# Key heads once in the projection weights of the two grouped attentions (640 columns, not 768), each key half written to both partition halves by ScalarE

## The chip, the cores and the metric

The kernel runs on one core of a Trainium2 chip. The metric is the device time of one execution in microseconds; three runs of the kernel before are shown, and the median counts.

## What is computed

The reference is two models in a row, on 512 tokens of width 1024, all in float32. The first has two layers of mixer and gated feed-forward. The second has two layers over 512 latent and 256 context tokens. In each of its layers one half of the mixer is a *grouped* attention: 8 query heads of 64 features share 2 key heads and 2 value heads. Layer 0 (even) has it as a banded window attention, layer 1 (odd) as a global block attention with normed and rotated queries and keys:

```python
def even_mixer(u_ctx, u_lat, w_in, w_out, a_prm, sink, rope_ang, need_ctx):
    p_ctx = u_ctx @ w_in
    p_lat = u_lat @ w_in
...
    qc, kc, vc = split_qkv(p_ctx[..., A_IN:], B_HEADS, B_KV_HEADS)
    ql, kl, vl = split_qkv(p_lat[..., A_IN:], B_HEADS, B_KV_HEADS)
...
def odd_mixer(u_ctx, u_lat, w_in, w_out, rpb, q_gain, k_gain, rope_ang, need_ctx):
...
    dq_c, dk_c, dv_c = split_qkv(p_ctx[..., C_IN:], D_HEADS, D_KV_HEADS)
    dq_l, dk_l, dv_l = split_qkv(p_lat[..., C_IN:], D_HEADS, D_KV_HEADS)
```

So a grouped projection has 512 query columns, 128 key columns (heads K0 and K1) and 128 value columns, each over a depth of 1024.

## The kernel before

**Tiles.** Tokens are counted as 768 columns, context first (256, `CTXS`) and latent behind it (512, `LAT`). A projected tensor lies with its features on the 128 partitions: `raw` of a grouped attention is `[128, 6, 768]`. Tiles 0 to 3 hold the queries, two heads in each, one on each half of the partitions. Tile 4 holds K0 on both halves and tile 5 holds K1 on both. The attention multiplies a query half by the key tile's rows of the same half (`raw[ROWS[half], j, ...]` with `k_tile(j)[ROWS[half], cols]`, and `k_tile` is `raw[:, 4 + j // 2, :]`), so that each key head must stand on both halves. For that the host function `grouped` lays the key columns out twice, 768 columns in all.

**The weight stream.** `WeightStream` brings all weights in a fixed order (`MAIN`) through a ring of 4 blocks; a block has up to 256 columns (1 MB), and SyncE loads the next one when the block 4 places before it is used up. A block is cut into pieces of 128 columns. Products are made of three float32r products: ScalarE casts a piece to its high part (`hi`), VectorE subtracts to get the low part (`lo`), into one of two slots, and TensorE multiplies high by high, high by low and low by high. `feature_products` runs over the pieces of a matrix: for each piece, for each segment of tokens, 8 row tiles by three products into one of 7 rotating banks; then it frees the piece's slot (`piece_used`).

**Side blocks.** Between the blocks of a host matrix come blocks of other matrices, the modulation weights (`SIDES`: `b_qk` and `d_qk` have three each, one behind each block of the host). VectorE multiplies such a block by two vectors and sums over its 8 row tiles (`sum_side`, 16 instructions); `sums_after` says behind which piece's `lo` this comes, for a side block behind the last piece of its host block. TensorE finishes it with 8 small products (`side_products`) behind the same piece. The modulation is read by later stages.

**The stage.** `qkv_stage` projects queries and keys piece by piece, then the values as one more piece, whose result TensorE transposes to token order. ScalarE runs in a fixed order: for piece j it first casts the weights of piece j + 1, then waits for piece j's products and copies its banks out, one copy for a segment. `b_qk` has both segments for the queries, `d_qk` only the latent one; keys and values have both in either. Behind the last copy of the values ScalarE casts the next stage's first piece (in `b_qk`), then copies the transposed values. The stage ends in a barrier of all engines. `c_qk` goes through the same function with ungrouped heads (`wide`).

Of the kernel before, what the change touches and what calls it, by code (L numbers as in the profile page):

```python
# [24 lines left out]
ACT = mybir.ActivationFunctionType  # L25
# [5 lines left out]
P = 128  # L31
# [21 lines left out]
HD = 64  # L53
# [16 lines left out]
NROT = 7  # L70
# [3 lines left out]
def feature_plan(n_cols, k_tiles=DK, width=256):  # L74

    return [(0, k_tiles, c, min(width, n_cols - c)) for c in range(0, n_cols, width)]


def token_plan(n_cols, k_tiles):

    return [(k, min(4, k_tiles - k), c, 512) for c in range(0, n_cols, 512) for k in range(0, k_tiles, 4)]
# [8 lines left out]
    ("up0", feature_plan(2 * FFN)), ("down0", token_plan(D, FK)),  # L90
    ("cv_in", feature_plan(2 * D)), ("cv_out", token_plan(D, DK)),
    ("up1", feature_plan(2 * FFN)), ("down1", token_plan(D, FK)),
    ("b_qk", feature_plan(768)), ("b_v", feature_plan(P, width=P)),
    ("lora", feature_plan(256) + [(0, DK, 256, P)]),
    ("rkv0", feature_plan(768)), ("rkv1", feature_plan(768)),
    ("out0", token_plan(D, DK)), ("ff1_0", feature_plan(DFF)), ("ff2_0", token_plan(D, DFF // P)),
    ("c_qk", feature_plan(1024)), ("c_v", token_plan(512, DK)),
    ("d_qk", feature_plan(768)), ("d_v", feature_plan(P, width=P)),
    ("out1", token_plan(D, DK)), ("ff1_1", feature_plan(DFF)), ("ff2_1", token_plan(D, DFF // P)),
]  # L100
ADAS = {"ada_mix0": ADA1, "ada_ffn0": ADA1, "ada_mix1": ADA1, "ada_ffn1": ADA1, "ada0": ADA2, "ada1": ADA2}
# [258 lines left out]
def build(nc, dram, out_dram, debug=None):  # L360

    psum = nc.alloc_psum_tensor("banks", [P, NBANK * BANK], F32)
    ps = [psum[:, i * BANK:(i + 1) * BANK] for i in range(NBANK)]
# [15 lines left out]
    @contextmanager  # L379
    def stage():  # L380
        with nc.cleanup_on_exit():  # L381
            yield
# [1146 lines left out]
    def flat_of(x):  # L1529

        return x[:].rearrange("p a b -> p (a b)")
# [180 lines left out]

    def qkv_stage(qk_name, v_name, hT, raw, n_q, vtok, q_segs, q_scale=1.0, then=None):

        n_k = raw.shape[1] - n_q
        v_cols = vtok.shape[2]
        wide = v_cols == BANK
        v_feat = flat_of(gate_rows)[:, 0:TOK]
        segs_of = lambda j: q_segs if j < n_q else [CTXS, LAT]
        with stage():  # L1720
            mm_done, copied, turned = sem("mm_done"), sem("copied"), sem("v_turned")
            first = weights.at["pe"]
            N = n_q + n_k
            n_copies = sum(len(segs_of(j)) for j in range(N))
            with nc.Block() as block:
                @block.sync
                def _(sp):
                    weights.load(sp, v_name)

                @block.tensor  # L1730
                def _(pe):
                    g = feature_products(pe, qk_name, hT, segs_of, copied)
                    if wide:
                        token_products(pe, v_name, all_tiles, lambda p, kk, i: tuple(
                            h[:, 2 * p + kk, i * P:(i + 1) * P] for h in hT), mm_done, copied, g0=g)
                    else:
                        g = feature_products(pe, v_name, hT, [CTXS, LAT], copied, g0=g)
                        pe.wait_ge(copied, g)
                        for t in all_tiles:
                            last = nc.tensor.transpose(ps[t // 4][:, (t % 4) * P:(t % 4 + 1) * P], v_feat[:, t * P:(t + 1) * P], ident[:])  # L1740
                        last.then_inc(turned, 1)

                @block.scalar
                def _(act):
                    g, hi_left = 0, N + (DK // 2 if wide else 1)
                    weights.hi(act)
                    hi_left -= 1
                    for j in range(N + (0 if wide else 1)):
                        if hi_left:
                            weights.hi(act)  # L1750
                            hi_left -= 1
                        act.wait_ge(weights.piece_used, first + j + 1)
                        for s in segs_of(j):
                            to = raw[:, j, s] if j < N else v_feat[:, s]
                            nc.scalar.activation(to, ps[g % NROT][:, 0:s.stop - s.start], ACT.Copy, scale=q_scale if j < n_q else 1.0).then_inc(copied, 1)
                            g += 1
                    if wide:
                        for _ in range(hi_left):
                            weights.hi(act)
                        if then is not None:  # L1760
                            weights.hi_early(act, then)
                        for t in all_tiles:
                            act.wait_ge(mm_done, t + 1)
                            nc.scalar.copy(vtok[:, t, :], ps[(g + t) % NROT][:]).then_inc(copied, 1)
                    else:
                        if then is not None:
                            weights.hi_early(act, then)
                        act.wait_ge(turned, 1)
                        nc.scalar.copy(vtok[:, 0:4, :], ps[0][:].rearrange("p (t d) -> p t d", d=P))
                        nc.scalar.copy(vtok[:, 4:TOK_T, :], ps[1][:, 0:2 * P].rearrange("p (t d) -> p t d", d=P))  # L1770

                @block.vector
                def _(dve):
                    for _ in range(N + (DK // 2 if wide else 1)):
                        weights.lo(dve)
                    if then is not None:
                        weights.lo_early(dve, then)
                    side_sums(dve, qk_name, v_name)
# [1434 lines left out]
def lay_out(i):  # L3213
    plans = dict(WEIGHTS)
    out = lay_out_first(i)
    i = {k: np.asarray(v) for k, v in i.items()}
    out.update(second_constants())
    unit = np.ones((P, DK), np.float32)
    for l in range(DEPTH):
        pre_mix, post_mix, pre_ff, post_ff = (columns(i[n][l]) for n in ("g_pre_mix_2", "g_post_mix_2", "g_pre_ff_2", "g_post_ff_2"))  # L3220
        out[f"gains_ada{l}"] = np.ascontiguousarray(np.concatenate([unit, pre_mix, post_mix, unit, pre_ff, post_ff], axis=1))
    for l in range(DEPTH):
        out[f"ada{l}"] = blocks_of(i["w_ada_2"][l], ADA2)
        out[f"out{l}"] = blocks_of(i["w_out_2"][l], plans[f"out{l}"])
        out[f"ff1_{l}"] = blocks_of(i["w_ff1_2"][l], plans[f"ff1_{l}"])
        out[f"ff2_{l}"] = blocks_of(i["w_ff2_2"][l], plans[f"ff2_{l}"])
    even, odd = i["w_in_even_2"][0], i["w_in_odd_2"][0]

    def grouped(w):

        k0, k1 = w[:, 512:512 + HD], w[:, 512 + HD:512 + 2 * HD]
        return np.concatenate([w[:, :512], k0, k0, k1, k1], axis=1), w[:, 640:768]

    qk, v = grouped(even[:, 1920:])
    out["b_qk"], out["b_v"] = blocks_of(qk, plans["b_qk"]), blocks_of(v, plans["b_v"])
    qk, v = grouped(odd[:, 1536:])
    out["d_qk"], out["d_v"] = blocks_of(qk, plans["d_qk"]), blocks_of(v, plans["d_v"])
    out["c_qk"], out["c_v"] = blocks_of(odd[:, :1024], plans["c_qk"]), blocks_of(odd[:, 1024:1536], plans["c_v"])
    out["lora"] = blocks_of(even[:, 1536:1920], plans["lora"])
    for h in range(2):  # L3240
        cols = [even[:, x * 512 + h * 256:x * 512 + (h + 1) * 256] for x in range(3)]
        out[f"rkv{h}"] = blocks_of(np.concatenate(cols, axis=1), plans[f"rkv{h}"])
    mu = np.stack([columns(i["a_mu_prev_2"][0]), columns(i["a_mu_next_2"][0])], axis=-1).reshape(P, 30)
    two = lambda x: np.concatenate([columns(x[0]), columns(x[1])], axis=1)
    out["r_cols"] = np.ascontiguousarray(np.concatenate([
        mu, two(i["a_w0_2"][0]), two(i["a_a0_2"][0]), columns(i["a_k_k_2"][0]), columns(i["a_k_a_2"][0]),
        columns(i["a_r_k_2"][0].reshape(-1)), columns(i["a_gn_w_2"][0]), columns(i["a_gn_b_2"][0])], axis=1))
    for name, src in (("w2", i["a_w2_2"][0]), ("a2", i["a_a2_2"][0])):
        full = np.zeros((2, P, 2, 2 * P), np.float32)
        for d in range(2):  # L3250
            for h in range(2):
                full[h, d * HD:(d + 1) * HD, d] = src[d][:, h * 256:(h + 1) * 256]
        out[name] = full
    out["g2"] = np.ascontiguousarray(i["a_g2_2"][0].reshape(P, 2, 2 * P).transpose(1, 0, 2))
    out["b_sink"] = i["b_sink_2"][0]
    out["rpb_table"] = rpb_layout(i["c_rpb_2"][0])
    out["d_gain"] = np.ascontiguousarray(np.stack([np.tile(i["d_q_gain_2"][0], 2), np.tile(i["d_k_gain_2"][0], 2)], axis=1))
    return out
# [13 lines left out]
```

## Time and profile before

| | us |
|---|---|
| runs of the kernel before | 3687.14, 3688.95, 3690.34 |
| their median | 3688.95 |
| span of the profiled execution, first to last instruction | 3684.6 |
| b_qk and b_v, TensorE's first product to the next stage's | 1339.8 to 1408.4 |
| d_qk and d_v | 2966.6 to 3022.7 |

The profiled execution's own device time is not listed beside its span; the median of the runs is 4.35 us above that span. A profile row names the line, the engine, the operation and the tile that is written and read. PE is TensorE, PEld its weight loads, DVE VectorE, ACT ScalarE, SP SyncE. Times in a timeline are from the start of the span. A matmul's duration includes its way through the array, so that the distance between two starts is what one costs.

### The profile page before, as it was taken

What the parts mean: (1) busy time and instruction counts of PE and PEld (TensorE: products, weight loads), DVE (VectorE), ACT (ScalarE), POOL (GpSimd) and SP (SyncE); (2) the same over time, 40 slices, a digit from 0 to 9 for tenths busy, and PEclk for the clock granted to TensorE, in tenths of its full rate; (3) what the DMA queues carried; (4) which work ended last, traced back from release to release, by engine and by line L of the source; (5) the groups of instructions that cost most, each with busy time, mean ns of one, the idle gap of its engine ahead of it and who ended that gap; (6) DMA issues with size and microseconds to landing.
All of it is one profiled execution on the core that took longest, in us unless ns stands there. A gap on an engine that the chain in (4) does not pass through costs nothing. (4 is left out here: it accounts for less than half of the span.)

```text
span 3684.6 us, 62774 instructions
## 1 busy us (share of the span) xinstructions
PE 3230.6 (88%) x26414; PEld 2617.1 (71%) x26414; DVE 2201.8 (60%) x3942; ACT 1289.6 (35%) x2191; POOL 139.9 (4%) x180
## 2 busy tenths in 40 slices
PE   6989998988999958976776777999998999879999
PEld 5767876646887757844765766887887777658787
DVE  7678866785786466766445445554334556663344
ACT  2333334334333332154324325222234225642243
POOL 0200001000000001000101100000000000000000
PEclk8989999998999979988988998999999999989999
DMA  7524462202335212310000022322221242022231
GB/s 291 166 105 182 183 182 88 69 12 78 135 137 138 99 48 105 125 53 30 5 32 12 5 72 82 113 103 98 75 92 58 103 138 70 1 97 92 82 96 69
DMA packets 64424, 342.67 MB, mean 93 GB/s; under 512 B 15120, under 2 KB 16656, under 8 KB 28432
## 3 DMA queue, kind: packets, MB, share of 16 engines
q1 hardware_dynamic: 61616, 326.82, 26.1%
q0 software_dynamic: 2528, 11.84, 0.9%
q8 instruction: 209, 3.42, 0.4%
q14 instruction: 71, 0.58, 0.1%
HBM read 327.84 MB, written 10.79 MB: 92 GB/s over the span
## 5 line engine op out<-in xcount | busy, mean ns | idle before, releaser
L263 DVE TENSOR_TENSOR weight_lo<-weight_ring,weight_hi 128x1024 fp32r<-128x1024 f32 x341 | 423.0, 1242 | 152.5 <-ACT weight_hi L248 147.6
L248 ACT CAST weight_hi<-weight_ring 128x1024 fp32r<-128x1024 f32 x341 | 355.9, 1044 | 177.4 <-PE banks L420 91.9
L418 PE MATMUL banks<-hT_hi.1,weight_hi 128*128 128x512 f32 x896 | 365.9, 408 | 24.8 <-PEq L381 22.7
L419 PE MATMUL banks<-hT_lo.1,weight_hi 128*128 128x512 f32 x896 | 358.8, 400 | 0.0
L420 PE MATMUL banks<-hT_hi.1,weight_lo 128*128 128x512 f32 x896 | 358.5, 400 | 0.0
L418 PEld LDWEIGHTS banks<-hT_hi.1,weight_hi 128*128 128x128 f32 x896 | 171.4, 191 | 68.2 <-issue 25.7
L419 PEld LDWEIGHTS banks<-hT_lo.1,weight_hi 128*128 128x128 f32 x896 | 171.3, 191 | 41.5 <-issue 1.9
L420 PEld LDWEIGHTS banks<-hT_hi.1,weight_lo 128*128 128x128 f32 x896 | 171.0, 191 | 41.9
L418 PE MATMUL banks<-hT_hi.3,weight_hi 128*128 128x512 f32 (+1 forms) x512 | 175.5, 343 | 7.9 <-PEq L381 7.9
L419 PE MATMUL banks<-hT_lo.3,weight_hi 128*128 128x512 f32 (+1 forms) x512 | 174.3, 341 | 0.0
L420 PE MATMUL banks<-hT_hi.3,weight_lo 128*128 128x512 f32 (+1 forms) x512 | 174.3, 340 | 0.0
L317 DVE SCALAR_TENSOR_TENSOR side_sum<-weight_ring,silu_c2.1,side_sum 128x256 f32<-128x256 f32 x336 | 160.3, 477 | 0.0
L317 DVE SCALAR_TENSOR_TENSOR weight_ring<-weight_ring,silu_c2.1 128x256 f32<-128x256 f32 x336 | 160.2, 477 | 0.0
L517 PE MATMUL banks<-weight_hi,left_hi.6 128*128 128x512 f32 x360 | 144.5, 401 | 8.3 <-DVE weight_lo L263 8.3
L520 PE MATMUL banks<-weight_lo,left_hi.6 128*128 128x512 f32 x360 | 142.5, 396 | 0.0
L519 PE MATMUL banks<-weight_hi,left_lo.6 128*128 128x512 f32 x360 | 141.9, 394 | 0.0
L317 DVE SCALAR_TENSOR_TENSOR weight_ring<-weight_ring,silu_c1.1 128x256 f32<-128x256 f32 x280 | 135.6, 484 | 10.5
L418 PE MATMUL banks<-hT_hi.2,weight_hi 128*128 128x256 f32 (+1 forms) x352 | 123.6, 351 | 17.1 <-PEq L381 17.1
L420 PE MATMUL banks<-hT_hi.2,weight_lo 128*128 128x256 f32 (+1 forms) x352 | 122.0, 347 | 0.0
L419 PE MATMUL banks<-hT_lo.2,weight_hi 128*128 128x256 f32 (+1 forms) x352 | 122.0, 346 | 0.0
L262 DVE TENSOR_TENSOR left_lo.6<-ff_hidden.1,left_hi.6 128x1536 fp32r<-128x1536 f32 x24 | 42.2, 1760 | 130.9 <-ACT weight_hi L248 130.9
L2666 ACT COPY residual.1<-banks 128x512 f32<-128x512 f32 x120 | 70.3, 586 | 140.6 <-PE banks L2824 139.4
(744 smaller groups left out, 7759.1 us busy)
## 6 DMA issues: line engine op xcount, KB each, us to landing
weight_ring<-ff SPq DMA_DIRECT2D x64, 1024.0 KB, 4.9
weight_ring<-ada SPq DMA_DIRECT2D x48, 1024.0 KB, 5.0
weight_ring<-up SPq DMA_DIRECT2D x44, 1024.0 KB, 6.9
weight_ring<-ada_ffn SPq DMA_DIRECT2D x24, 1024.0 KB, 5.0
weight_ring<-down SPq DMA_DIRECT2D x20, 1024.0 KB, 4.9
weight_ring<-ada_mix SPq DMA_DIRECT2D x16, 1024.0 KB, 4.9
first_blocks.1<-ada_mix SPq DMA_DIRECT2D x8, 1024.0 KB, 11.8
weight_ring<-cv_in SPq DMA_DIRECT2D x8, 1024.0 KB, 5.0
```

Of the source, the lines that this page charges most:

```text
L248: self.nc.scalar.copy(hi, raw).then_inc(self.hi_made, 1)
L262: self.nc.vector.tensor_tensor(x[2], x[0], x[1].bitcast(F32), ALU.subtract)
L263: self.nc.vector.tensor_tensor(lo, raw, hi.bitcast(F32), ALU.subtract).then_inc(self.lo_made, 1)
L317: ins = self.nc.vector.scalar_tensor_tensor(out=to, in0=w[:, k, :], scalar=vec[:, k, v:v + 1], in1=to, op0=ALU.mult, op1=ALU.add)
L418: nc.tensor.matmul(out, w_hi, x_hi, start=first, stop=False)
L419: nc.tensor.matmul(out, w_hi, x_lo, start=False, stop=False)
L420: return nc.tensor.matmul(out, w_lo, x_hi, start=False, stop=last)
L517: one = nc.tensor.matmul(out, xh, hi[:, kk, :], start=(k == 0), stop=False)
L519: nc.tensor.matmul(out, xl, hi[:, kk, :], start=False, stop=False)
L520: last = nc.tensor.matmul(out, xh, lo[:, kk, :], start=False, stop=(k == k_tiles - 1))
L2666: nc.scalar.copy(XT_flat[c % 2], pair(c, X_AT, 4 * CH)).then_inc(xt_copied[c % 2], 1)
```

## The change

The host function `grouped` takes the key columns once (K0 and K1 side by side, 640 columns with the queries). `b_qk` and `d_qk` have blocks of 256, 256 and 128 columns and five pieces. In `qkv_stage` a grouped attention has one key piece. When its products are in, ScalarE writes for each segment four copies of 64 partitions each: rows 0 to 63 of the bank (K0) to both halves of tile 4, and rows 64 to 127 (K1) to both halves of tile 5. The last of the four signals `copied` for that bank. `raw` and all that reads it are as before.

```diff
--- before.py
+++ after.py
@@ -90,12 +90,12 @@
     ("up0", feature_plan(2 * FFN)), ("down0", token_plan(D, FK)),
     ("cv_in", feature_plan(2 * D)), ("cv_out", token_plan(D, DK)),
     ("up1", feature_plan(2 * FFN)), ("down1", token_plan(D, FK)),
-    ("b_qk", feature_plan(768)), ("b_v", feature_plan(P, width=P)),
+    ("b_qk", feature_plan(640)), ("b_v", feature_plan(P, width=P)),
     ("lora", feature_plan(256) + [(0, DK, 256, P)]),
     ("rkv0", feature_plan(768)), ("rkv1", feature_plan(768)),
     ("out0", token_plan(D, DK)), ("ff1_0", feature_plan(DFF)), ("ff2_0", token_plan(D, DFF // P)),
     ("c_qk", feature_plan(1024)), ("c_v", token_plan(512, DK)),
-    ("d_qk", feature_plan(768)), ("d_v", feature_plan(P, width=P)),
+    ("d_qk", feature_plan(640)), ("d_v", feature_plan(P, width=P)),
     ("out1", token_plan(D, DK)), ("ff1_1", feature_plan(DFF)), ("ff2_1", token_plan(D, DFF // P)),
 ]
 ADAS = {"ada_mix0": ADA1, "ada_ffn0": ADA1, "ada_mix1": ADA1, "ada_ffn1": ADA1, "ada0": ADA2, "ada1": ADA2}
@@ -1712,9 +1712,13 @@
 
     def qkv_stage(qk_name, v_name, hT, raw, n_q, vtok, q_segs, q_scale=1.0, then=None):
 
-        n_k = raw.shape[1] - n_q
         v_cols = vtok.shape[2]
         wide = v_cols == BANK
+
+
+        n_k = raw.shape[1] - n_q if wide else 1
+        spread_k = [(0, 0, 0), (0, 1, 0), (1, 0, 1), (1, 1, 1)]
+        rows_of = (slice(0, HD), slice(HD, P))
         v_feat = flat_of(gate_rows)[:, 0:TOK]
         segs_of = lambda j: q_segs if j < n_q else [CTXS, LAT]
         with stage():
@@ -1751,8 +1755,14 @@
                             hi_left -= 1
                         act.wait_ge(weights.piece_used, first + j + 1)
                         for s in segs_of(j):
-                            to = raw[:, j, s] if j < N else v_feat[:, s]
-                            nc.scalar.activation(to, ps[g % NROT][:, 0:s.stop - s.start], ACT.Copy, scale=q_scale if j < n_q else 1.0).then_inc(copied, 1)
+                            bank = ps[g % NROT][:, 0:s.stop - s.start]
+                            if n_q <= j < N and not wide:
+                                for tile, dst, src in spread_k:
+                                    last = nc.scalar.copy(raw[rows_of[dst], n_q + tile, s], bank[rows_of[src]])
+                                last.then_inc(copied, 1)
+                            else:
+                                to = raw[:, j, s] if j < N else v_feat[:, s]
+                                nc.scalar.activation(to, bank, ACT.Copy, scale=q_scale if j < n_q else 1.0).then_inc(copied, 1)
                             g += 1
                     if wide:
                         for _ in range(hi_left):
@@ -3228,8 +3238,7 @@
 
     def grouped(w):
 
-        k0, k1 = w[:, 512:512 + HD], w[:, 512 + HD:512 + 2 * HD]
-        return np.concatenate([w[:, :512], k0, k0, k1, k1], axis=1), w[:, 640:768]
+        return w[:, :640], w[:, 640:768]
 
     qk, v = grouped(even[:, 1920:])
     out["b_qk"], out["b_v"] = blocks_of(qk, plans["b_qk"]), blocks_of(v, plans["b_v"])
```

## Rows read from the trace of the kernel before

**Rows 1.** Page, part 1: busy us, share of the span, instructions

```profile
PE 3230.6 (88%) x26414; PEld 2617.1 (71%) x26414; DVE 2201.8 (60%) x3942; ACT 1289.6 (35%) x2191; POOL 139.9 (4%) x180
```

**Rows 2.** Busy time cut into windows, b_qk stage; the first row names columns

```profile
core 0: us, PE busy (x) PEld busy (x) DVE busy (x) ACT busy (x) POOL busy (x), PEclk, DMA share, GB/s
1339.80:1351.00 11.20, 11.13 (x49) 10.04 (x50) 7.38 (x17) 1.05 (x1) 0.00 (x0) 0.75 0.29 96
1386.40:1394.70 8.30, 8.30 (x51) 7.22 (x49) 1.30 (x2) 1.79 (x4) 0.00 (x0) 1.00 0.01 2
1394.70:1404.00 9.30, 9.26 (x55) 7.84 (x54) 0.00 (x0) 0.86 (x2) 0.00 (x0) 1.00 0.46 169
```

**Rows 3.** Timeline of TensorE, key piece K1 of b_qk; start, us

```profile
1386.17 0.28 PE L418 MATMUL banks<-hT_hi.2,weight_hi 128*128 128x256 f32 x1
...
1393.79 0.40 PE L418 MATMUL banks<-hT_hi.2,weight_hi 128*128 128x512 f32 x1
1394.03 0.39 PE L419 MATMUL banks<-hT_lo.2,weight_hi 128*128 128x512 f32 x1
...
1394.49 0.28 PE L429 MATMUL banks<-ones.1,side_sum 128*128 128x1 f32 x2
...
1395.30 0.36 PE L418 MATMUL banks<-hT_hi.2,weight_hi 128*128 128x256 f32 x1
```

**Rows 4.** Timeline of TensorE, key piece K1 of d_qk

```profile
3000.97 0.28 PE L418 MATMUL banks<-hT_hi.4,weight_hi 128*128 128x256 f32 x1
...
3009.41 0.28 PE L429 MATMUL banks<-ones.1,side_sum 128*128 128x1 f32 x2
```

**Rows 5.** Waits, 1339 to 1408 us: total us, times, longest

```profile
PE banks L418 <- PEq L381: 7.9, 1, 7.9
...
PE banks L1740 <- ACT gate_rows.1 L1755: 1.0, 1, 1.0
```

**Rows 6.** Timeline of ScalarE, b_qk stage from 1377 us

```profile
1377.90 1.05 ACT L248 CAST weight_hi<-weight_ring 128x1024 fp32r<-128x1024 f32 x1
1386.37 0.87 ACT L1755 ACTIVATE qk_b.1<-banks 128x256 f32<-128x256 f32 x2 [7.42 <-PE banks L420]
1387.13 1.05 ACT L248 CAST weight_hi<-weight_ring 128x1024 fp32r<-128x1024 f32 x1
1394.69 0.87 ACT L1755 ACTIVATE qk_b.1<-banks 128x256 f32<-128x256 f32 x2 [6.51 <-PE banks L420]
1404.00 0.87 ACT L1755 ACTIVATE gate_rows.1<-banks 128x256 f32<-128x256 f32 x2 [8.44 <-PE banks L420]
```

**Rows 7.** Groups by line and form, ScalarE, 1340 to 1408 us: mean ns

```profile
L1755 ACT ACTIVATE qk_b.1<-banks 128x512 f32<-128x512 f32 x6 | 3.6, 593 | 0.0
L1755 ACT ACTIVATE qk_b.1<-banks 128x256 f32<-128x256 f32 x6 | 2.3, 383 | 44.7 <-PE banks L420 44.7
```

**Rows 8.** Timeline of VectorE, d_qk stage

```profile
2988.65 1.22 DVE L263 TENSOR_TENSOR weight_lo<-weight_ring,weight_hi 128x1024 fp32r<-128x1024 f32 x1
2993.45 1.23 DVE L263 TENSOR_TENSOR weight_lo<-weight_ring,weight_hi 128x1024 fp32r<-128x1024 f32 x1 [3.58 <-ACT weight_hi L248]
2994.59 0.35 DVE L315 TENSOR_SCALAR side_sum<-weight_ring,silu_c2.1 128x256 f32<-128x256 f32 x1
...
3000.39 0.48 DVE L317 SCALAR_TENSOR_TENSOR weight_ring<-weight_ring,silu_c2.1 128x256 f32<-128x256 f32 x1
```

**Rows 9.** Timeline of SyncE's queue, d_qk stage

```profile
2980.46 0.33 SPq L219 DMA_DIRECT2D weight_ring<-ada  x1
```

**Rows 10.** DMA issues by line, 2966 to 3022 us: count, KB, us to landing

```profile
weight_ring<-ada SPq DMA_DIRECT2D x3, 1024.0 KB, 5.4
```

**Rows 11.** Waits of TensorE, whole kernel: total us, times, longest

```profile
PE banks L418 <- PEq L381: 62.7, 10, 7.9
```

**Rows 12.** Busy time in a window, the scan stages; columns as rows 2

```profile
1566.00:2280.00 714.00, 523.68 (x13348) 434.07 (x13348) 374.72 (x973) 294.46 (x707) 53.49 (x110) 0.90 0.11 36
```

**Rows 13.** Mean granted clock of TensorE over the span

```profile
core 0: 3684.6 us, clock 0.941
```

## The prediction

> **What bounds the kernel now.** I read the busy shares first: TensorE is busy for 3230.6 of the 3684.6 us span, 88% of it, while ScalarE and VectorE are far below it [rows 1]. A share of the whole kernel says nothing about the two stages that the change touches, so the second view is the busy time cut at the piece borders of the first grouped stage (b_qk with b_v, some 68 us of the span). A piece is 128 weight columns: TensorE is busy in 8.30 of 8.30 us of the sixth key-and-query piece and in 9.26 of 9.30 us of the value piece that follows, both at granted clock 1.00 (the 2.4 GHz level). In the sixth piece VectorE works 1.30 us and ScalarE 1.79 us, and hardly any data is moved [rows 2]. Third, the waits of that stretch: inside the stage TensorE waits only at its start, behind the barrier (7.9 us), and for 1.0 us ahead of the transposes at its end, for ScalarE's copy of the values [rows 5]. No matmul of a piece waits for a weight, a bank or a transfer. So TensorE's stream of products sets the length of the stage, and what is taken out of that stream in the middle comes off the end, if ScalarE's new work stays inside its idle time.
>
> **What is removed.** The key heads stand in the weights twice, so tiles 4 and 5 of the six are a piece of K0|K0 and one of K1|K1. After the change there is one piece K0|K1 in each of the two grouped stages (b_qk and d_qk). A key piece covers 8 row tiles, 3 products, 2 segments (256 context and 512 latent tokens): 8 x 3 x 2 = 48 matmuls with 48 weight loads. In b_qk the sixth piece's first matmul starts at 1386.17 and the side product behind its last one at 1394.49: 8.32 us [rows 3]. In d_qk the same two marks are 3000.97 and 3009.41: 8.44 us [rows 4]. Both pieces are keys over both segments, so the removed work is the traced one and not a mean of mixed shapes (a query piece of d_qk has only 24 matmuls). The sum of the gain is 8.32 + 8.44 = 16.76 us.
>
> The trace spaces two 512-column matmuls of this piece by 0.24 us (1393.79 to 1394.03) [rows 3], and the 8.32 us are with such spacings. The Trainium skill, "TensorE: Matmul & The Clock Gate", section "Back-to-back issue gap", gives about 131 ns for sustained 512-column matmuls and, for an isolated one, columns over 2.4 GHz plus 2.5 ns, which is 109 ns at 256 columns; with the one for 24 matmuls and the other for 24 the two pieces would be worth 2 x (24 x 0.131 + 24 x 0.109) = 11.5 us. The trace does not agree, and since it times the very instructions that go, 16.76 us stands.
>
> **What goes with it at no price.** One weight split in each stage goes: a cast on ScalarE (about 1.05 us) and a subtraction on VectorE (about 1.22 us). Both engines wait for TensorE here, so this is worth nothing. The third weight block is 512 KB where it was 1024 KB; nothing in the stage waits for a transfer [rows 5], so nothing again. The number of blocks stays at three for each stage, so the same number of side blocks (parts of the modulation product, summed on VectorE) goes with them, and their side products stay on TensorE: 0.81 us from 1394.49 to 1395.30 [rows 3] is kept.
>
> **What is added on ScalarE.** The key piece is now read out eight times in half height (two segments, two tiles, two halves) where each of the two old pieces was read out twice in full height. A full-height copy takes 383 ns with 256 columns and 593 ns with 512 [rows 7]; the pair of them takes 0.76 us until the next instruction starts (1386.37 to 1387.13) [rows 6]. No row shows a copy of 64 partitions, nor one that moves values to the other half. Bounds: at half price the eight take 4 x 0.38 = 1.5 us; one after the other without any overlap 4 x (0.383 + 0.593) = 3.9 us. I take 4 x 0.76 = 3.0 us, by the same line's own pair, since a row of 256 or 512 columns is still walked over in full. This lies beside TensorE's side products and value piece: from the start of the key copies to that of the value copies there are 9.31 us (1394.69 to 1404.00) in which ScalarE does nothing but 0.87 us of copies [rows 6]. The next weight cast is not queued behind the key copies: the value piece's cast is issued ahead of them, in the place of the one at 1377.90 [rows 6]. What is queued behind them is the pair of value copies, and TensorE's transposes wait for those. So the added copies cost nothing up to 9.31 us in all, 1.16 us for each, three times the 256-column row. No matmul bank waits either: in b_qk the value piece's banks only ask for copies of the third query piece. Cost on the path: 0, between 0 and 0. Below nothing is excluded, since the path does not run through this engine.
>
> **What is moved on VectorE.** The third side sum came after the sixth subtraction and now comes after the fifth, and the value piece's subtraction comes behind it. I look at d_qk, where query pieces are short and VectorE is tighter. The fifth subtraction starts at 2988.65 and takes 1.22 us; the side sum ran from 2994.59 to 3000.39 + 0.48 = 3000.87, that is 6.28 us [rows 8]. Put together it runs from 2989.9 to 2996.2, and TensorE asks for it at 3000.97, the end of the key piece: 4.8 us to spare. The value piece's subtraction is then over by 2997.4 and is asked for at about 3001.8, after the side products. Its cast takes the place of the cast that released the subtraction at 2993.45 [rows 8]. The sum needs its side block: issued at 2980.46 [rows 9], 5.4 us to land [rows 10], there at 2985.9, 4.0 us ahead. On SyncE the later loads wait either for what is unchanged in time or for events that come one piece earlier. So nothing here is late, and the cost is 0. If this cover were gone, TensorE would stand still at the side products by the time that is missing, at most 8.4 us in a stage.
>
> **After the stages.** Each ends at a barrier and the next begins with weights that are in the ring already; those loads were issued before the border or come earlier with it. The attentions read the same four copies of the keys from the same places. So the shift is carried to the end. The profiled execution's span goes from 3684.6 to 3667.8 us. The median of the runs shown is 3688.95 us, 4.35 us above that span; I keep this distance: 3688.95 - 16.76 = 3672.2 us.
>
> **The rivals.**
> (a) *One stage gives its gain back*: a side sum, a transfer or ScalarE is late by a piece there. Speaking for it: only that VectorE's work of two blocks now stands closer together in d_qk. Against it: the 4.8 and 4.0 us to spare. Time: 3688.95 - 8.4 = 3680.6 us.
> (b) *The copies across partition halves are dear.* From 9.31 us on they push the value copies, the transposes and the barrier. The gain is gone when eight take 9.31 + 8.38 = 17.7 us, 2.2 us each, four to six times the rows of full height [rows 7]. Time 3689 us; the same time stands for the case that products are not in fact taken out. Nothing speaks for either.
> (c) *The clock, slower than before.* TensorE starts each stage at the lower level: the first piece of b_qk had granted clock 0.75 over 11.20 us, where a warm piece needs 8.3 [rows 2]. There are ten such starts of the projections alone [rows 11], and the scan stages further on run at 0.90 in the mean over 714 us with TensorE at 524 busy [rows 12]. If the shift by one piece changes what the clock does behind each barrier and in the scan, the mean clock moves. TensorE's 3230.6 us at 0.941 mean clock [rows 1, 13] are worth 3.4 us for each 0.001. The gain is gone when the mean falls by 0.005, and the kernel is slower by over 7.4 us when it falls by 0.007, to 0.934: 3696.4 us. Against it: the three runs, in which the clock had its own freedom, lie within 3.2 us.
> (d) *The clock, the other way*: a mean higher by 0.002 gives 3665 us.
> The Trainium skill, same page, section "What's actually happening", says that the activity monitor behind the clock is free-running and that the number of slow matmuls at a start varies from run to run; by that rule (c) and (d) would be scatter and not a step, and no row of one profile can show it.
>
> **How the numbers follow.** The forecast, both pieces off the path, has a chance of 0.82; its own range is 3667 to 3678 us: 16.76 us with 5 us on either side, for scatter of the clock (the 3.2 us between runs and the 2.7 us that one cold first piece costs). Rival (a) has 0.06, (b) 0.04, (c) 0.03, (d) 0.05. The range is 3667 to 3679 us; it leaves out most of (a) to (d), 0.18. A measurement can tell about 0.2% from no change, 7.4 us, so that the border of faster is 3681.6 us: faster 0.82 + 0.06 + 0.05 = 0.93, the same 0.04, slower 0.03.
>
> **What would show it.** TensorE's instructions fall by 96, each grouped stage has five projection pieces ahead of the value piece, and b_qk's stage is shorter by 8.3 us and d_qk's by 8.4. ScalarE shows eight copies in a row of about 0.38 and 0.59 us in each, done 6 us ahead of the value copies. TensorE's wait ahead of the transposes stays at 1.0 us; if it grows, (b) is at work. A wait of the side products for VectorE would be (a). If the stages shrink as said and the time does not, the mean granted clock tells whether it is (c), and the stretches between the marks tell where. The prediction is wrong if copies to the other half cost over 1.16 us each or if a stage behind the barriers was waiting for something that did not move with it.

## The result, and the profile after

The changed kernel took 3669.78 us in the median of four runs (3668.07 to 3672.60), the kernel before 3689.64 us in that session: a ratio of 0.9947 with a 95% interval of 0.9935 to 0.9959, that is 19.9 us less (15 to 24). The forecast was 3672.2 us, a gain of 16.8.

The page of the changed kernel, its head and part 1; it answers [rows 1]:

```profile
span 3668.9 us, 62580 instructions
...
PE 3212.3 (88%) x26318; PEld 2598.4 (71%) x26318; DVE 2200.5 (60%) x3940; ACT 1292.5 (35%) x2197; POOL 139.9 (4%) x180
```

TensorE lost 96 matmuls (26414 to 26318) and 18.3 us of busy time. ScalarE has six instructions more (sixteen half-height copies in place of eight full-height ones, and two casts fewer).

The timeline of ScalarE in the b_qk stage of the changed kernel (start us, duration us); it answers [rows 6]:

```profile
1379.16 1.05 ACT L248 CAST weight_hi<-weight_ring 128x1024 fp32r<-128x1024 f32 x1
1387.71 3.89 ACT L1761 COPY qk_b.1<-banks 64x256 f32<-64x256 f32 x8 [7.50 <-PE banks L420]
1396.94 0.87 ACT L1765 ACTIVATE gate_rows.1<-banks 128x256 f32<-128x256 f32 x2 [5.34 <-PE banks L420]
1397.70 1.05 ACT L283 CAST weight_hi<-weight_ring 128x1024 fp32r<-128x1024 f32 x1
```

The eight copies stand in a row, 3.89 us, and ScalarE is then idle for 5.34 us until the value products are ready. The value piece's cast (1379.16) is ahead of them. The waits of the same stage of the changed kernel (total us, times, longest), which answer [rows 5]:

```profile
PE banks L418 <- PEq L381: 7.9, 1, 7.9
...
PE banks L1744 <- ACT gate_rows.1 L1765: 1.0, 1, 1.0
```

They are what they were: 7.9 us at the barrier, 1.0 us ahead of the transposes. TensorE has no new wait. The timeline of VectorE in the d_qk stage of the changed kernel; it answers [rows 8]:

```profile
2982.67 1.22 DVE L263 TENSOR_TENSOR weight_lo<-weight_ring,weight_hi 128x1024 fp32r<-128x1024 f32 x1
2983.81 0.35 DVE L315 TENSOR_SCALAR side_sum<-weight_ring,silu_c2.1 128x256 f32<-128x256 f32 x1
...
2990.00 1.22 DVE L263 TENSOR_TENSOR weight_lo<-weight_ring,weight_hi 128x1024 fp32r<-128x1024 f32 x1
2995.97 0.17 DVE L449 TENSOR_TENSOR modulation_ada1.1<-banks,bias_ada1.1 128x6 f32<-128x6 f32 x1 [4.75 <-PE banks L429]
```

The fifth subtraction, the third side sum and the value piece's subtraction (2990.00) follow each other without a pause, and VectorE then waits 4.75 us for the side products behind the key piece.

**Where the time went.** The program has barriers, and TensorE's first instruction behind each is a mark that both kernels have. Lengths between marks, in us, for the kernel before, and the difference to it in each profile taken since (the two of the further version are given in its paragraph):

| stretch | before | after | both_again | both_third | both_fourth | before_again | b_only | d_only | copies_alone | copies_x4 |
|---|---|---|---|---|---|---|---|---|---|---|
| b_qk stage | 68.52 | -8.41 | -8.56 | -8.43 | -8.35 | -0.04 | -8.33 | +0.02 | -0.02 | -1.62 |
| lora stage | 35.70 | -0.91 | -1.04 | -0.91 | -0.89 | -0.01 | -0.88 | 0.00 | -0.01 | -0.86 |
| d_qk stage | 56.04 | -8.47 | -8.48 | -8.48 | -8.46 | -0.01 | +0.02 | -8.47 | +0.01 | -1.05 |
| all the rest | 3524.4 | +2.1 | -4.6 | -6.5 | -8.1 | -4.1 | +1.9 | +0.6 | +1.9 | -0.1 |
| span | 3684.64 | -15.7 | -22.7 | -24.3 | -25.8 | -4.2 | -7.3 | -7.9 | +1.9 | -3.6 |

The first three rows repeat to 0.2 us in profiles of one kernel. The fourth does not: it moves by 4.1 us between two profiles of the kernel before (before and before_again), by 6.0 us if copies_alone, whose three stages have their old lengths, is taken in, and by 10 us among the four of the changed one.

### The profile page after: what moved, and what is told of

Its sections match the earlier page's. It is cut to its first block and busy times, and to the rows that moved or that the text cites. A ratio compares the mean times of both kernels' runs of the same rounds, so it can differ in the third digit from the quotient of the medians.

```text
span 3668.9 us, 62580 instructions
## 1 busy us (share of the span) xinstructions
PE 3212.3 (88%) x26318; PEld 2598.4 (71%) x26318; DVE 2200.5 (60%) x3940; ACT 1292.5 (35%) x2197; POOL 139.9 (4%) x180
## 5 line engine op out<-in xcount | busy, mean ns | idle before, releaser
L418 PE MATMUL banks<-hT_hi.1,weight_hi 128*128 128x512 f32 x896 | 365.2, 408 | 25.7 <-PEq L381 23.5
```

Of the source, the lines that this page charges most:

```text
L418: nc.tensor.matmul(out, w_hi, x_hi, start=first, stop=False)
```

## The experiments

Ten runs were made in three sessions; each session has its own runs of the kernel before to compare with. The edits are shown against the changed kernel, in cuts marked by dots.

| | ratio to before | 95% interval | difference of the medians, us |
|---|---|---|---|
| both_again | 0.9936 | 0.9923 to 0.9948 | -23.5 |
| b_only | 0.9974 | 0.9964 to 0.9983 | -10.0 |
| copies_alone | 0.9996 | 0.9988 to 1.0005 | -1.0 |
| copies_x4 | 0.9985 | 0.9976 to 0.9994 | -6.5 |
| both_third | 0.9938 | 0.9925 to 0.9950 | -24.6 |
| d_only | 0.9981 | 0.9972 to 0.9990 | -6.6 |
| before_again | 0.9999 | 0.9990 to 1.0008 | +0.3 |
| values_first | 0.9939 | 0.9926 to 0.9953 | -23.0 |
| both_fourth | 0.9938 | 0.9925 to 0.9950 | -22.7 |
| values_second | 0.9945 | 0.9931 to 0.9959 | -21.3 |

**The changed kernel again.** No edit.

> The changed kernel itself, unaltered, against the kernel before, to size the effect. First theory: only the two removed key pieces count, 8.3 + 8.4 = 16.8 us, a ratio of 0.9954; the 19.9 us between the first medians are partly scatter of the clock. Rival: something else gives another 3 us, then the ratio stays at 0.9946 or below and the stretches outside the two stages are shorter by 3 us in sum.

Measured: 23.5 us, and the interval (19 to 28) leaves 16.8 out. The two stages were shorter by 8.56 and 8.48 us, the lora stage between the changed places by 1.04. So the pieces are worth what was said, and something more is there.

**One stage alone.** In b_only the second host layout and the second stage stay as before:

```diff
-    ("d_qk", feature_plan(640)), ("d_v", feature_plan(P, width=P)),
+    ("d_qk", feature_plan(768)), ("d_v", feature_plan(P, width=P)),
...
-        n_k = raw.shape[1] - n_q if wide else 1
+        once = qk_name == "b_qk"
+        n_k = 1 if once else raw.shape[1] - n_q
...
-                            if n_q <= j < N and not wide:
+                            if n_q <= j < N and once:
```

> Only b_qk has its key heads once, d_qk keeps 768 columns and six pieces. If the gain is the piece taken out of each stage and nothing further on, this gives half of it: 8.4 us of the kernel before (ratio 0.9977), the b_qk stage shorter by 8.4 us, the d_qk stage as before (56.0 us from its first product to the first score of the attention). Rival, that the shift itself changes the clock or the stages behind: the gain would be away from half of both_again by more than 2 us.

Measured: -10.0 us (6 to 13), b_qk stage -8.33, d_qk stage unchanged. It is half of the 19.9 of the first session, but both_again's half would be 11.8; that is 1.8 away, just within its bound of 2 us. d_only is the mirror of it (640 columns and one key piece in d_qk alone).

> Only d_qk has its key heads once; b_qk keeps 768 columns. Pieces alone: 8.4 us, ratio 0.9977, and with b_only the two make up the whole. Rival, an extra behind the d_qk stage: 12 to 14 us, ratio 0.9965, and the stretch from the ungrouped attention's start to the next attention's is 113 to 117 us, against 119 in the kernel before and in b_only.

Measured: -6.6 us (4 to 10), d_qk stage -8.47, and from the ungrouped attention's start to the next one's 120.9 us. That speaks against an extra behind d_qk: a kernel that has the whole change there has the longest such stretch of the profiles, and copies_alone (next paragraph), whose d_qk stage keeps its length, has one of 115.0 us. The two ratios multiply to 0.9955, 16.6 us, which is the sum of the forecast; with the intervals of both put together that is 12 to 21 us.

**ScalarE's part alone.** The weights keep 768 columns, laid out as queries, K0|K1, K0|K1; all six pieces are multiplied, and of the sixth one column of each bank is read:

```diff
-    ("b_qk", feature_plan(640)), ("b_v", feature_plan(P, width=P)),
+    ("b_qk", feature_plan(768)), ("b_v", feature_plan(P, width=P)),
...
-        n_k = raw.shape[1] - n_q if wide else 1
+        n_k = raw.shape[1] - n_q
...
-                            if n_q <= j < N and not wide:
+                            if j == n_q and not wide:
...
+                            elif j == n_q + 1 and not wide:
+                                col = 0 if s.start == 0 else 1
+                                nc.scalar.copy(spare[:, col:col + 1], bank[:, 0:1]).then_inc(copied, 1)
...
-        return w[:, :640], w[:, 640:768]
+        return np.concatenate([w[:, :640], w[:, 512:640]], axis=1), w[:, 640:768]
```

> ScalarE's part alone: the weights stay at 768 columns with K0|K1 twice and all six pieces are multiplied, the first key piece is read out by the eight half-height copies, and of the second one only one column of each bank is read. If the copies are hidden, the time is that of the kernel before within 2 us (ratio 0.9995 to 1.0005). Rival, that eight copies in a row (3.9 us) hold up something: slower than before by up to 2 x 3 us, ratio 1.0015 or more.

Measured: -1.0 us, with an interval that holds 1. The stages have their old lengths to 0.02 us. So the eight copies are hidden here. They stand one piece earlier than in the changed kernel, and what is queued behind them is the value piece's cast (at 1392.09, right behind the last copy) and not the value copies; that they are hidden in their real place too is read from the changed kernel's own wait ahead of the transposes, 1.0 us as before. What the two stages became shorter is then the removed products.

**The limit of the cover.** Each of the eight copies is done four times, one waiting for the other:

```diff
                                 for tile, dst, src in spread_k:
+                                    for _ in range(3):
+                                        nc.scalar.copy(raw[rows_of[dst], n_q + tile, s], bank[rows_of[src]]).then_inc(again, 1)
+                                        repeats[0] += 1
+                                        act.wait_ge(again, repeats[0])
                                     last = nc.scalar.copy(raw[rows_of[dst], n_q + tile, s], bank[rows_of[src]])
```

> The changed kernel, but every one of the eight half-height copies is done four times, one behind the other. The prediction's limit: they are free up to 9.3 us in a stage. 32 copies take 16 x 0.38 + 16 x 0.59 = 15.5 us, with the waits between them up to 18 us, so the value copies come 6.3 to 8.7 us late and the kernel is 12.6 to 17.4 us slower than both_again: about the time of the kernel before. TensorE's wait ahead of the transposes grows from 1.0 us to 7 to 10 us in each stage. Rival, that ScalarE has more room than thought (its copies are not what the transposes wait for): within 3 us of both_again.

Measured: 16.9 us slower than both_again in the same session (3682.9 against 3666.0), inside the 12.6 to 17.4 expected. The timeline of ScalarE in the b_qk stage of copies_x4, first key copies, last one, value copies:

```profile
1386.07 1.16 ACT L1763 COPY qk_b.1<-banks 64x256 f32<-64x256 f32 x3 [7.42 <-PE banks L420]
...
1401.51 0.58 ACT L1766 COPY qk_b.1<-banks 64x512 f32<-64x512 f32 x1
1402.11 0.87 ACT L1770 ACTIVATE gate_rows.1<-banks 128x256 f32<-128x256 f32 x2
```

and the wait of TensorE ahead of the transposes there:

```profile
PE banks L1745 <- ACT gate_rows.1 L1770: 7.7, 1, 7.7
```

32 copies take 16.0 us (1386.07 to 1402.11); TensorE waits 7.7 us where it waited 1.0. The cover is real and has an end: 16.0 less the 6.7 us of added wait leaves 9.3 us that are free, which is the 9.31 us read off [rows 6]. The wait in the d_qk stage is 7.7 us as well. Per stage the price over both_again was 6.9 and 7.4 us, 14.4 in all; the other 2.5 of the 16.9 us lie outside the two stages.

**The kernel before against itself, and the changed one a third and a fourth time.**

> The kernel before, unaltered, against itself: what the timing shows where nothing is changed, and a second profile of it. Scatter theory: ratio 1 within its interval, and the stretch from the ungrouped attention to the next one, 119.2 us in the first profile, comes out anywhere between 113 and 119. Rival, extra behind the changed d_qk stage: that stretch is 119 again within 1 us.

> The changed kernel once more, beside d_only and the kernel before in one session, since the gain came out at 19.9 and 23.5 us and not 16.8. The two removed pieces measured 8.4 and 8.5 us in the traces; in the traces so far the stretches between barriers elsewhere differ by up to 6 us from one profile to the next, in kernels that are the same there. If the rest is this scatter, the ratio comes back towards 0.9954 and, over the three sessions, lies between 0.994 and 0.9955. Rival: a true extra of 3 to 6 us behind the d_qk stage (the ungrouped attention and the norm stage), then the ratio is 0.9945 or below again.

> The changed kernel a fourth time, as the neighbour of values_second in one session and for the size of the gain. The pieces give 16.8 us and the earlier rise of the clock behind the b_qk stage 0.9 us, 17.7 in all (0.9952); the three sessions so far gave 19.9, 23.5 and 24.6 us. If the rest is scatter, this one comes out at 0.994 to 0.9955, and the profile shows the lora stage 0.9 us shorter again, with the clock's rise 3.1 to 3.5 us behind its start, not 5.3.

Measured: before_again has the ratio 0.9999 and a second profile whose span is 4.2 us shorter than the first; from the ungrouped attention to the next 118.3 us, so by its own bound of 1 us this run did not tell scatter from an extra. both_third and both_fourth gave 0.9938 twice. For both_third that falls on the side of its rival, an extra of 3 to 6 us (0.9945 or below), though not at the place that it named: d_only and copies_alone speak against that. Both are a little below the 0.994 to 0.9955 that scatter alone would have given, and their intervals end at 0.9950, short of the 0.9952 of the parts. So in three of four sessions the gain is 22.7 to 24.6 us, and the parts make 17.7. The lora stage of both_fourth was 0.89 us shorter, as expected.

**A further version.** values_first has the value piece first, then the key piece, then the queries; the transposes of the values are issued ahead of the last query piece, and the next stage's first cast ahead of its copies:

```diff
-    ("b_qk", feature_plan(640)), ("b_v", feature_plan(P, width=P)),
+    ("b_v", feature_plan(P, width=P)), ("b_qk", feature_plan(640)),
...
+                    def turn(piece):
+                        if piece != n_q - 1:
+                            return
+                        pe.wait_ge(copied, G + 2 - NROT)
+                        for t in all_tiles:
+                            last = nc.tensor.transpose(turned_to[t // 4][:, (t % 4) * P:(t % 4 + 1) * P], v_feat[:, t * P:(t + 1) * P], ident[:])
+                        last.then_inc(turned, 1)
+
+                    g = feature_products(pe, v_name, hT, [CTXS, LAT], copied)
+                    feature_products(pe, qk_name, hT, lambda piece: segs_of(piece + 1), copied, g0=g, after_piece=turn)
...
+                        if j == n_pieces - 1:
+                            if then is not None:
+                                weights.hi_early(act, then)
+                            act.wait_ge(turned, 1)
```

> A further version: the value piece comes first in both grouped stages, then the key piece, then the queries; the transposes of the values are issued ahead of the last query piece and the next stage's first weight cast too. In the changed kernel 4.4 us (b) and 3.7 us (d) lie between the end of the value products and the next stage's first product: copies, transposes, copies, cast and split, barrier. Behind a query piece only its copy, the side products, the modulation's sum and the barrier are left: some 2.4 us in each. Theory: another 3.3 us faster than the changed kernel. Rival, VectorE's third side sum now ends last in d_qk, where three short query pieces follow each other: then the gain there is gone and the whole is within 1.5 us of the changed kernel or slower.

> The version with the value piece first again, since one session gave it the same time as the changed kernel although its trace has three places that are shorter: b_qk stage by 2.6 us, lora stage by 1.6 us (TensorE's pause at the barrier is short and the clock stays at its upper level), d_qk stage by 1.6 us. Theory: 5 to 6 us faster than both_fourth, ratio 0.9925 to 0.9945. Rival: the same places are shorter and the time is not, because what is saved comes back in the scan and attention stages, whose lengths move by some us with the clock; then within 2 us of both_fourth.

Measured: values_first was expected to gain another 3.3 us, from the two stages alone. The places are shorter in both profiles, by more than that: against the kernel before, the b_qk stage by 10.98 and 10.98 us, the lora stage by 2.50 and 2.49, the d_qk stage by 10.04 and 9.99, some 5.7 us in all beyond the changed kernel. The time is not: 0.9939 beside 0.9938 for both_third, 0.9945 beside 0.9938 for both_fourth. In the profiles the second half of the scan took, first both_fourth, then values_second (busy time cut at the barriers; columns as rows 2):

```profile
1902.24:2144.11 241.87, 175.79 (x6152) 153.10 (x6153) 114.02 (x281) 88.09 (x213) 24.79 (x52) 0.92 0.06 18
```

```profile
1901.88:2148.41 246.53, 175.12 (x6152) 153.89 (x6153) 114.37 (x281) 87.89 (x213) 24.38 (x52) 0.92 0.06 18
```

4.7 us longer with the same instructions and the same busy time, so what was saved is not seen in that profile's span; the first half of the scan adds another 3.7 us. Two profiles cannot say that it is always so: the kernel before (245.6 us) and copies_alone (246.0) have a second half as long. The version is no better than the changed kernel within what these runs can tell.

## Why the prediction was right, and where it was short

**The removed pieces**: right. 8.32 and 8.44 us were read off the kernel before [rows 3, 4]; the stages shrank by 8.35 to 8.56 and 8.46 to 8.48 us in four profiles, and by 8.33 and 8.47 us where one stage was changed alone. The estimate from the Trainium skill's spacing ("TensorE: Matmul & The Clock Gate", "Back-to-back issue gap") was 11.5 us for both; the trace and the runs, with 16.8 to 17.0 us, disagree with it.

**What goes at no price, and VectorE's move**: right. No new wait of TensorE. The third side sum was expected to end 4.8 us ahead of its need in d_qk. It ended by 2990.00, where the next subtraction starts, and ScalarE's first key copy, right behind the key products, starts at 2995.18: some 5 us. The sum itself began at 2983.81 without a pause, so its side block had landed.

**ScalarE's copies**: the cost on the path (0) and the limit (9.31 us) were right, the size was not: 3.0 us were taken, and 3.89 us measured, the upper bound. The mis-sized step is "by the line's own pair": full-height copies of two banks start 0.28 us apart where one takes 0.38, the half-height ones do not. Three of them in the changed kernel, one by one:

```profile
1387.71 0.37 ACT L1761 COPY qk_b.1<-banks 64x256 f32<-64x256 f32 x1 [7.50 <-PE banks L420]
...
1388.09 0.36 ACT L1761 COPY qk_b.1<-banks 64x256 f32<-64x256 f32 x1
...
1388.47 0.37 ACT L1761 COPY qk_b.1<-banks 64x256 f32<-64x256 f32 x1
```

They start 0.38 us apart. Two more views of the same trace narrow down why: the fourth and fifth copies together, and the two full-height copies of the transposed values.

```profile
1388.85 0.97 ACT L1761 COPY qk_b.1<-banks 64x256 f32<-64x256 f32 x2
...
1398.78 0.59 ACT L1779 COPY v_b.1<-banks 128x512 f32<-128x512 f32 x1
1399.26 0.38 ACT L1780 COPY v_b.1<-banks 128x256 f32<-128x256 f32 x1
```

The fourth and fifth read different banks and still take 0.97 us together, no less than 0.367 + 0.582, so it is not the shared bank. The last two are plain copies of full height and start 0.48 us apart where the first takes 0.59, so it is not the other instruction either. What is left of these is the half height; no run changed it alone. It costs nothing here.

**"I keep this distance"**: this step was wrong in its reason. The 4.35 us between span and median were taken as something that lies around the span. In the changed kernel the profiled run has its own time beside its span, 3670.81 and 3668.9 us, and in its other three runs too the time is 1.9 us above the span. The profiled execution of the kernel before was then one of some 3686.5 us, 2.4 us below the median of its runs. Set against that, the first profile pair shows a gain of only 15.7 us. A single span is a sample of what moves by some us. The forecast of the median was not hurt by it: the gain is taken off the median of the runs, and the distance drops out.

**"So the shift is carried to the end"**: this is the step that fell short. The stage right behind b_qk, lora, became 0.9 us shorter in every profile with a shortened b_qk stage (six of those in the table) and by 0.01 us or less in the others. Nothing was changed in it. Its first piece in the kernel before and in d_only, busy time in the first 5.5 us (columns as rows 2; the last but two is the granted clock):

```profile
1408.39:1413.90 5.51, 5.51 (x25) 5.49 (x26) 4.60 (x12) 1.05 (x1) 0.00 (x0) 0.52 0.70 198
```

```profile
1410.35:1415.90 5.55, 5.55 (x26) 5.51 (x27) 4.64 (x12) 1.05 (x1) 0.00 (x0) 0.52 0.67 207
```

the same in the changed kernel, in copies_x4 and in values_second:

```profile
1401.35:1406.90 5.55, 5.55 (x29) 5.35 (x30) 4.65 (x12) 1.04 (x1) 0.00 (x0) 0.69 0.70 211
```

```profile
1406.50:1412.00 5.50, 5.50 (x29) 5.32 (x30) 4.60 (x12) 1.05 (x1) 0.00 (x0) 0.68 0.65 213
```

```profile
1399.34:1404.90 5.56, 5.56 (x36) 5.07 (x37) 4.65 (x12) 1.05 (x1) 0.00 (x0) 1.00 0.92 323
```

The granted clock is at its lower level (1.2 GHz) early in this stage and rises to 2.4 GHz on the way: 5.3 us behind the start in the kernel before, before_again, d_only and copies_alone, 3.1 to 3.5 us behind it in the four profiles of the changed kernel, in b_only and in copies_x4. It fell 1.5 us ahead of the start in the first group, and in the changed kernel and b_only between 0.3 us ahead of it and 0.05 us behind it. The granted clock is 0.50 throughout 1406.90:1413.72 in the kernel before and 1401.40:1404.81 in the changed one, 6.8 and 3.4 us. The rise can be seen in the starts of the 256-column matmuls, which go from 0.21 to 0.12 us apart; in the changed kernel:

```profile
1404.42 0.41 PE L420 MATMUL banks<-hT_hi.2,weight_lo 128*128 128x256 f32 x1
1404.64 0.36 PE L418 MATMUL banks<-hT_hi.2,weight_hi 128*128 128x256 f32 x1
1404.84 0.28 PE L419 MATMUL banks<-hT_lo.2,weight_hi 128*128 128x256 f32 x1
1404.96 0.28 PE L420 MATMUL banks<-hT_hi.2,weight_lo 128*128 128x256 f32 x1
```

1.8 to 2.2 us sooner at double speed is 0.9 to 1.1 us, against a measured difference of 0.86 to 1.04. copies_x4, whose b_qk stage is shorter by only 1.62 us, shows it too, so it does not grow with the length that is saved; there the clock had already fallen 6.7 us ahead of the start, in TensorE's long wait for ScalarE. Every kernel with the early rise also lacks the sixth piece in b_qk, so no run separates the shift of the stage's end from the missing piece itself. In values_second the clock did not fall at that barrier: another 1.6 us. The end of the b_qk stage and the start of the next in the changed kernel, then the start in values_second:

```profile
1397.87 0.88 PE L1744 MATMUL banks<-identity.1,gate_rows.1 128*128 128x128 f32 x6 [0.96 <-ACT gate_rows.1 L1765]
1401.35 0.50 PE L418 MATMUL banks<-hT_hi.2,weight_hi 128*128 128x256 f32 x1 [2.60 <-PEq L381]
```

```profile
1399.34 0.36 PE L418 MATMUL banks<-hT_hi.2,weight_hi 128*128 128x256 f32 x1 [1.38 <-PEq L381]
```

TensorE paused 1.4 us there and not 2.6. But the transposes are gone from that place as well: the changed kernel has 4.4 us between its last product and the next stage's first, of which 0.9 us are transposes. Which of the two kept the clock up was not tried. The forecast had the clock as rivals (c) and (d) and took it for scatter; at this place it is a step that repeats. The Trainium skill, "TensorE: Matmul & The Clock Gate", section "What's actually happening", has the monitor free-running and the count of slow matmuls varying from run to run; over ten profiles the rise at this place has two groups and not a spread, so the trace does not agree with it here, while in the scan and the ungrouped attention, below, the lengths do vary.

**What stays open.** The pieces and the lora stage make 17.7 us. The medians say 20 to 25 in four sessions. Between the two lies "all the rest" of the table: -8.1 to +2.1 us in the changed kernel, -4.1 to +1.9 us in the three profiles whose stages have their old lengths. A large part of it is in two stretches, the scan's second half (241.4 to 246.8 us) and the one from the ungrouped attention to the next (113.4 to 120.9 us). For the second, d_only and then both_fourth:

```profile
3012.77:3133.65 120.88, 103.96 (x884) 80.81 (x885) 78.29 (x201) 62.90 (x139) 7.58 (x6) 0.87 0.25 76
```

```profile
3001.61:3115.38 113.77, 98.14 (x885) 75.93 (x885) 78.22 (x201) 62.80 (x139) 7.59 (x6) 0.92 0.26 80
```

Same instructions, mean granted clock 0.87 and 0.92: TensorE's busy time differs by 5.8 of the 7.1 us. So in this pair the stretch goes with the clock. That the shift moves the clock there on average in the changed kernel's favour fits the medians, but b_only and d_only together show only 16.6 us, and with four profiles against three it is argued, not shown. Within one session the step from b_only to both_again was 13.5 us and the one from d_only to both_third 18.0 us, where a piece makes 8.5 and a piece with the lora stage's share 9.3; so the extra appears where both stages are changed, and no run says why. The mean clock over all runs of a kernel in a session does not settle it: 0.9428 against 0.9427 for the kernel before in the session of both_again, 0.9436 against 0.9425 with both_third and 0.9432 against 0.9428 with both_fourth, for gains of 23.5, 24.6 and 22.7 us.

That the first time fell well inside the range of 3667 to 3679 us is in part luck. Taken off the 3688.95 us from which the forecast started, the gains of the three later sessions would be 3664.4 to 3666.3 us, just below it. The terms that were read off the rows are right; what is beyond them had been put at nothing but scatter.

**The rivals.** (a), a stage gives its gain back: did not happen, and its cover of 4.8 us was found. (b), dear copies: refuted by copies_alone and by the unchanged wait of 1.0 us; copies_x4 shows where it would begin. (c), slower by the clock: no. (d), faster by the clock: the 0.9 us are of this kind, and perhaps the rest.

The price that (c) and (d) put on the clock, 3.4 us for each 0.001 of the mean, is not borne out. The profile of the changed kernel has 0.943 where the one before has 0.941, which at that price would be 6.9 us on top of the pieces, and the spans differ by 15.7 us, less than the pieces. In the session of both_again ten runs of the kernel before share the mean 0.942 and lie between 3684.0 and 3695.3 us. Two smaller sums of the prediction are off, without weight for the forecast: a mean lower by 0.007 makes the kernel slower by 7.3 us at its own price, not by over 7.4, and a cold first piece costs 11.20 - 8.3 = 2.9 us by its own rows, not 2.7.

## What to carry to other kernels

Read a removal off the very instructions that go, with starts and not durations, and check it by the length between two barriers, which repeats to 0.2 us where the whole kernel moves by 5 us or more. Give an added chain of copies the time until the next thing that is queued behind it, and test the limit by multiplying the chain: here the 9.3 us of cover were found again to 0.1 us. And where TensorE pauses at barriers, look at the granted clock behind the next barrier as a term of its own: its rise there moved by 2 us with the stage ahead, and in the version with a pause of 1.4 us and no transposes ahead of it, it did not fall at all.

## What the runs showed of the hardware

A ScalarE copy of 64 partitions takes nearly as long as one of 128: 0.367 and 0.582 us in the mean (256 and 512 columns) against 0.383 and 0.593 [rows 7], and 0.38 and 0.59 for the plain full-height copies above. Writing to the other half of the partitions costs nothing extra: the copies of the 256-column segment, two within a half and two across, start 0.38 us apart. The mean of ScalarE's half-height forms in the changed kernel (count, busy us, mean ns):

```profile
L1761 ACT COPY qk_b.1<-banks 64x512 f32<-64x512 f32 x4 | 2.3, 582 | 0.1
L1761 ACT COPY qk_b.1<-banks 64x256 f32<-64x256 f32 x4 | 1.5, 367 | 7.5 <-PE banks L420 7.5
```

Two more things were not expected. The clock's rise behind the b_qk stage came at one of two distances from the barrier, 5.3 or 3.1 to 3.5 us, by whether the stage ahead had six pieces or five. And unchanged stages move by some us from one execution to the next: the stretch from the ungrouped attention to the next one by 3.2 us among the four profiles of the changed kernel, and by 7.4 us over the profiles of all kernels.
